# The weights' rings 128 bytes, for 64, further into a row of 1 KB than the moving buffers

## What is computed

```python
D_MODEL = 1024; SEQ = 256; DEPTH = 2; D_FF = 2816
def swiglu(h, w_gate, w_up, w_down):
    return (jax.nn.silu(h @ w_gate) * (h @ w_up)) @ w_down
for l in range(DEPTH):                      # first block
    x = x + rms_norm(parallel_mixer(rms_norm(x, ...), ...), ...)
    x = x + rms_norm(memory_cross_attention(rms_norm(x, ...), mem_n, ...), ...)
    x = x + rms_norm(swiglu(rms_norm(x, ...), w_gate[l], w_up[l], w_down[l]), ...)
for l in range(DEPTH):                      # second block
    x = x + 0.5 * swiglu_2(rms_norm_2(x, ...), ...)
    h = rms_norm_2(x, ...)                  # three attention branches, gated and merged
    x = x + merged @ w_out[l]
    x = x + 0.5 * swiglu_2(rms_norm_2(x, ...), ...)
```

## Time and profile before

| | us |
|---|---|
| median of 3 runs | 2378.32 |
| lowest and highest | 2377.19, 2390.8 |
| the profiled execution | 2388.41 |
| its span, first to last instruction | 2387.1 |

### The profile page before, as it was taken

How to read it: one execution, slowest core, us unless ns; L and a number is a source line. 1 busy time by engine, 2 the same in 40 slices (tenths; PEclk the granted TensorE clock), 3 DMA queues, 4 the chain that set the end, 5 groups by cost and what they waited for, 6 DMA issues and landing times.

```text
span 2387.1 us, 40450 instructions
## 1 busy us (share of the span) xinstructions
PE 2174.9 (91%) x17158; PEld 2082.6 (87%) x17158; DVE 1425.2 (60%) x2190; ACT 1131.8 (47%) x1744; POOL 95.4 (4%) x95
## 2 busy tenths in 40 slices
PE   6977889979887799799988988999999988988999
PEld 6866879979777799799988877999999988878999
DVE  5555566555546666565565656665665674667664
ACT  4554444444544444344444555544444444465442
POOL 4100010000000000000000000000000000000000
PEclk9888999989899999999998998999999998999999
DMA  6423346735233356546544223556555542234654
GB/s 212 150 80 115 105 138 214 220 120 185 98 107 97 111 195 206 175 159 190 197 143 142 89 82 113 177 183 202 169 186 186 181 154 89 89 107 142 195 185 150
DMA packets 98484, 360.30 MB, mean 151 GB/s; under 512 B 11136, under 2 KB 11149, under 8 KB 97920
## 3 DMA queue, kind: packets, MB, share of 16 engines
q1 hardware_dynamic: 96192, 349.22, 45.2%
q0 software_dynamic: 1680, 5.35, 0.7%
q10 hardware_dynamic: 432, 3.15, 0.3%
HBM read 356.61 MB, written 3.43 MB: 151 GB/s over the span
## 4 chain that ended last, share of the span: by engine, by line
PE 74%; DVE 14%; ACT 8%; issue 3%; POOL 1%; DMA 0%; ACTq 0%; DVEq 0%; SPq 0%; POOLq 0%
PE bank L274 66%; DVE w_lo L1270 3%; ACT w_hi L785 2%; PE bank L328 1%; DVE xn_lo L1292 1%; DVE sq L1327 1%; PE bank L310 1%; POOL sq L1884 1%; PE bank L645 1%; DVE x L1331 1%; PE bank L333 1%; PE bank L329 1%; DVE sq L1840 1%; PE bank L618 0%; DMA raw<-in_stream 0%
## 5 line engine op out<-in xcount | busy, mean ns | idle before, releaser
L1270 DVE TENSOR_TENSOR w_lo<-raw,w_hi 128x1024 fp32r<-128x1024 f32 x664 | 806.8, 1250 | 431.7 <-ACT w_hi L785 431.0
L274 PE MATMUL bank<-xn_hi,w_hi 128*128 128x256 f32 x3168 | 902.9, 285 | 95.0 <-DVE xn_lo L1292 81.8
L274 PE MATMUL bank<-xn_lo,w_hi 128*128 128x256 f32 x3168 | 894.2, 282 | 0.0
L274 PE MATMUL bank<-xn_hi,w_lo 128*128 128x256 f32 x3168 | 893.6, 282 | 0.0
L785 ACT ACTIVATE w_hi<-raw 128x1024 fp32r<-128x1024 f32 x664 | 671.4, 1049 | 236.8 <-PE bank L274 233.9
L274 PEld LDWEIGHTS bank<-xn_hi,w_hi 128*128 128x128 f32 x3168 | 608.5, 192 | 108.0 <-issue 105.9
L274 PEld LDWEIGHTS bank<-xn_hi,w_lo 128*128 128x128 f32 x3168 | 608.7, 192 | 0.0
L274 PEld LDWEIGHTS bank<-xn_lo,w_hi 128*128 128x128 f32 x3168 | 608.1, 192 | 0.2
L274 PE MATMUL bank<-hid_hi,w_hi 128*128 128x256 f32 x1056 | 295.0, 279 | 0.0
L274 PE MATMUL bank<-hid_lo,w_hi 128*128 128x256 f32 x1056 | 295.0, 279 | 0.0
L274 PE MATMUL bank<-hid_hi,w_lo 128*128 128x256 f32 x1056 | 295.0, 279 | 0.0
(11 more groups left out here) (344 smaller groups left out, 2764.1 us busy)
## 6 DMA issues: line engine op xcount, KB each, us to landing
raw<-in_stream SPq DMA_DIRECT2D x664, 512.0 KB, 4.2
skew<-vec POOLq DMA_DIRECT2D x12, 192.0 KB, 4.2
table<-skew POOLq DMA_DIRECT2D x1, 1408.0 KB, 7.2
con<-in_con ACTq DMA_DIRECT2D x1, 1029.0 KB, 14.9
x<-in_x ACTq DMA_DIRECT2D x1, 1024.0 KB, 6.8
xn<-in_mem ACTq DMA_DIRECT2D x1, 1024.0 KB, 11.3
out<-x SPq DMA_DIRECT2D x4, 256.0 KB, 3.4
logit<-in_small POOLq DMA_DIRECT2D x3, 288.5 KB, 3.0
```

The costliest lines, as they stand in the source:

```text
L274: m = T.matmul(out, a, b, start=first and j == 0, stop=True, skip_group_check=True)
L1270: V.tensor_tensor(w_lo[m % RING], raw[m % RING], w_hi[m % RING].bitcast(F32), ALU.subtract).then_inc(*lo_done.next())
```

## The change

The unused tensor in front of the rings is twice as long, 128 bytes for 64. The rings `raw`, `w_hi` and `w_lo` and all that is allocated after them begin 64 bytes further; the rings now begin 256 bytes into a row of 1 KB, the activations still 128. No instruction, no wait and no order is changed.

```diff
-    sb("offset", [P, 16])
+    sb("offset", [P, 32])
     raw = [sb(f"raw{r}", [P, HK, COLS]) for r in range(RING)]
     w_hi = [sb(f"w_hi{r}", [P, HK, COLS], F32R) for r in range(RING)]
     w_lo = [sb(f"w_lo{r}", [P, HK, COLS], F32R) for r in range(RING)]
```

## The result

| | before | after |
|---|---|---|
| median, us | 2377.19 (5 runs, 2370.31 to 2390.8) | 2415.42 (5 runs, 2411.97 to 2430.04) |
| the profiled execution, us | 2388.41 | 2430.04 |
| its span, us | 2387.1 | 2428.7 |

The changed kernel takes 1.016 times as long (95% interval 1.012 to 1.020): 38 us more. The forecast was 2,378, with a range up to 2,408.

What follows compares the result with a forecast made beforehand. The prediction took TensorE, busy for 91% of the span, as the bound. It costed every moved part at 0 us on the profiled 2,388.4 and forecast a median of 2,378, range 2,343 to 2,408.

Steps and rivals of the forecast that it cites:

- The bound: TensorE, busy for 91% of the span; six feed-forward pieces of 1,488 matmuls hold 1,039.8 of 2,387.1 us.
- The two paces: Feed-forward pieces take 168.9 or 175.5 us, 113.5 or 117.9 ns a matmul; the move was costed at nothing in both.
- the sign named for it: In `products`, one weight load of three takes 192 ns at the slow pace, read as overhead between the two reads.
- The step that failed: TensorE's matmuls: paces the same for every distance in the trace, so the move costs 0 us in both.
- the sign that the prediction named last: The forecast fails if the offset itself sets the pace of TensorE's matmuls, and not the restart.
- rival D: All 14,600 matmuls: reads collide more, a step of 4.4 ns above the slow pace; 90 us more, 2,468; chance 0.04.
- B: Six pieces and mixers' runs: wider distance favours the slow pace; 26 us more, 2,414 profiled, 2,404 median; chance 0.16.
- "Six slow, 281 ns everywhere": Sign in the profile after that the wider distance favours the slow pace: six slow pieces, every matmul at 281 ns.
- A: TensorE's matmuls: wider distance favours the quick pace; all quick is 39 us less than profiled, median 2,346; chance 0.20.
- C: All matmuls: 128 bytes keep the two reads apart, 106.7 ns each; 138 us less on the median, 2,240; chance 0.04.
- the sign from `mem_hi`: `mem_hi` matmuls: median 276 ns as moving operand, none under 278 as stationary, so never quick; address weighs on pace.
- The spread of the runs: Whole kernel: two layers more or less at the slow pace make 13 us, so the scatter was read as both paces.

Runs made afterwards that it cites:

- moved_reads: Changed kernel with every buffer in place, but slot_T and feed-forward matmuls read their moving operand 64 bytes further on (wrong numbers); 2,380.3 us once.
- e2_all_moved: Against the kernel before, 64 bytes put in front of everything, so rings and activations both move and their distance stays 64; ratio 1.002 (0.997 to 1.006).
- the strided runs: Kernel before and changed kernel with the two column tiles of a weight row interleaved, the stationary piece every other number; 2,433.1 and 2,452.2 us.
- short loads: Changed kernel, but in slot_T and the feed-forward layers two of three weight loads take 32 columns for 128; 2,394.3 us once.

## Why the prediction was wrong

**The bound, right.** The six pieces in which only TensorE counts are where half of the loss sits, and the busy time of L274, 45.5 us longer, covers the whole loss. ScalarE, VectorE, the DMAs and what lies behind the rings were costed at nothing and cost nothing: 1,044 and 1,224 ns, 4.1 us, ratio 0.998.

**The two paces, read rightly as such,** and as a matter of the two reads, which moved_reads shows. That the sign named for it, the stretch of a weight load from 188 to 192 ns, led there was partly luck: at 192 bytes the same pace of 117.9 ns has every load at 187 or 188, and so has the kernel before in `slot_rows`. So "at the slow pace every matmul has 281" holds for the four slow pieces and not for the pace.

**The step that failed** is this one: the paces "were the same for every distance that occurs in the trace. I therefore cost the move at nothing in the two paces". The distances in the trace were 64, 576, -64 and -576. I counted them as four. With a period of 256 bytes they are two, 64 (576 is 2 x 256 + 64) and its opposite; the trace held no other sample, and 128 is neither. The argument that all six layers have the same offset and yet two paces was sound for what it said, that the offset does not choose between the two; it says nothing on whether another offset has the same two. The runs showed that it has not: 176.8 us at 128 for 168.9 and 175.5. It is the sign that the prediction named last, that the offset itself sets the pace. I should have asked how many different distances the evidence held modulo anything, and given "a pace of its own" more than the 0.04 of rival D.

**The rivals.** B had the right side and nearly the size (2,404 on the median, 2,414 on the profiled execution; 2,415 and 2,430 measured), by the wrong mechanism: it had the stream lock into the slow pace of 175.5 us, and the pieces have 176.8, a third pace. In its terms: 13.2 us for the two quick pieces, right; 6 x 1.3 = 8.0 us for the step above the slow pace, not in B; and 20.5 for its 12.5 us between the pieces, of which 0.9 ns x 5,700 = 5 us is the same step again; the other 3 are within the scatter of the runs. The direction of D (a worse pace) was right with a step of 0.9 ns where it had 4.4. "Six slow, 281 ns everywhere" would have been read as B on the median duration alone; the lengths of the pieces told the difference. A and C are out, and so is the sign from `mem_hi` as I read it. A wider distance isn't better, and "never quick" was too much to read out of one tile: the very trace that was read has `slot_rows` at the quick pace from 578 to 587 us, as the line under moved_reads shows, and in e2_all_moved, at the same distances, matmuls with `mem_hi` stationary have a minimum of 276 ns.

**The spread of the runs** was read as the mix of the two paces. That can't be all of it: the profiled run of the changed kernel is its slowest, 2,430, with 176.8 us in all six pieces, the quicker of the two lengths seen at 128, and another run took 2,412.

**The Trainium skill** (page "SBUF — State Buffer", section "Who interferes with whom") gives TensorE two independent read ports and says PE never waits; by it the distance could not matter. The measurement decides: 168.9 to 183.8 us for the same 1,488 matmuls, by the distance and the restart alone. The page "TensorE: Matmul & The Clock Gate", section "Back-to-back issue gap", has 109.2 ns for 256 columns (N / 2.4 + 2.5), and calls this the gap of an isolated matmul; the prediction took it for a stream with a weight load each. No piece of 1,488 matmuls in any run here came under 113.5.

**What stays open.** Why these distances have these paces is not settled: the picture of one read overtaking the other did not bring its quicker pieces in the strided runs, where the stride or the 4 bytes may hide it, and with short loads five sixths of the overhead stay. Nor is it settled what decides, after a wait, between the two paces of 64 and of 128, or how often each comes at 192. No kernel here beat the one before clear of noise.

## What to carry to other kernels

Where matmuls with a weight load each follow one another at full clock, work out the distance from start to start from a long piece of the chain, and compare it with columns / 2.4 GHz; the difference here was 7 to 17 ns of 107 and depended on where the stationary and the moving operand begin relative to each other. Try the relative offset in steps of 64 bytes up to 256 and measure (64 was best here, 0 and 256 worst, by 2.4%), move both rings of a split operand alike, and leave absolute positions alone. When a trace is used to argue that an address does not matter, first count how many different values of it the trace really holds.

## What the runs showed that was not expected

- The same program at the same clock holds one of two paces over 1,488 matmuls (168.9 or 175.5 us) and chooses anew after a wait; distances 48 and 128 have several paces too (175.5, 176.3, 183.8; 176.8, 178.8).
- 4 bytes of distance (60 for 64) cost 2.6 us of 175.5 against the slow pace and 9.1 against the quick one.
- The worst pace of all the distances tried was at 48 bytes, not at 0: 123.5 ns a matmul in two of six pieces.
- At half the clock none of this shows: 213 ns from start to start in the kernel before and in the changed one.
